# Twelve weight low parts move from GpSimd to VectorE, and VectorE's order changes in two mixers

## The reference, cut to what matters

```python
x = x + 0.5 * (silu(n @ w_gate) * (n @ w_up)) @ w_down   # n = rmsnorm(x), width 2816
p = rmsnorm(x) @ w_in
z = gelu(p[..., :512]); u, v = z[..., :256], z[..., 256:]
v = group_layernorm(v, v_norm, 4)                # 4 groups of 64
sv = einsum('gts,bnsgd->bntgd', w_s * tril, v) + b_s
y_a = u * sv
y_b = bg * shortconv(cg * xin)
y_c = silu(g) * group_layernorm(retention(rotary(q), rotary(k), v), gn, 4)
x = x + concat(y_a, y_b, y_c) @ w_out
x = x + 0.5 * swiglu(rmsnorm(x))                 # again width 2816
```

## Time and profile before

| what | value |
|---|---|
| median of 3 runs | 3357.05 us (3355.66 to 3357.43) |
| profiled execution, its own time | 3355.51 us |
| its span, first to last instruction | 3353.9 us |
| TensorE busy | 3236.1 us, 96% |
| VectorE busy | 2029.2 us, 61% |
| ScalarE busy | 1457.0 us, 43% |
| GpSimd busy | 906.4 us, 27% |
| mean granted TensorE clock | 0.992 |

### The profile page before, as it was taken

The page is one execution under the profiler, slowest core; times in us unless marked ns, Lnnn a source line. Parts: engine busy times, 40 slices in busy tenths (PEclk is TensorE's granted clock), DMA queues, the critical chain, the costliest instruction groups (busy, mean ns, idle before and its releaser), DMA issues.

```text
span 3353.9 us, 47772 instructions
## 1 busy us (share of the span) xinstructions
PE 3236.1 (96%) x20092; PEld 2874.7 (86%) x20092; DVE 2029.2 (61%) x2997; ACT 1457.0 (43%) x2244; POOL 906.4 (27%) x413
## 2 busy tenths in 40 slices
PE   8999999999989999999999999999999999999998
PEld 6887899978668899888999778899899998788998
DVE  6568755445856544575747636574775576366656
ACT  4465445433534444354434324453454343235433
POOL 3210133321400333203232431323232323313232
PEclk9999999999999999999999999999999999999999
DMA  4310333331102333313222322332332323223332
GB/s 131 112 43 26 107 97 117 103 100 58 63 26 88 101 113 101 124 56 123 89 88 95 113 84 77 117 101 82 114 101 86 105 85 122 76 89 107 94 96 76
DMA packets 239815, 308.97 MB, mean 92 GB/s; under 512 B 8337, under 2 KB 168097, under 8 KB 239089
## 3 DMA queue, kind: packets, MB, share of 16 engines
q1 hardware_dynamic: 236016, 291.41, 27.1%
q0 software_dynamic: 3584, 14.52, 1.2%
HBM read 303.80 MB, written 2.10 MB: 91 GB/s over the span
## 4 chain that ended last, share of the span: by engine, by line
PE 78%; DVE 16%; ACT 3%; issue 1%; DMA 0%; POOL 0%; DVEq 0%; ACTq 0%
PE bank L595 24%; PE bank L597 24%; PE bank L596 24%; DVE wlo L2074 3%; ACT whi L1318 1%; DVE wraw L2096 1%; DVE raw_w L2096 1%; PE bank L974 1%; DVE xl L2147 1%; PE bank L615 1%; PE bank L1257 1%; PE bank L1248 1%; DVE ul_w L2274 1%; PE bank L1182 0%; DVE st L2105 0%
## 5 line engine op out<-in xcount | busy, mean ns | idle before, releaser
L3128 POOL TENSOR_TENSOR wlo<-wraw,whi 128x1024 fp32r<-128x1024 f32 (+3 forms) x217 | 555.0, 2561 | 1508.0 <-ACT whi L1318 1507.6
L595 PE MATMUL bank<-xh,whi 128*128 128x256 f32 (+1 forms) x2456 | 724.6, 295 | 48.6 <-DVE zt L2269 20.0
L1318 ACT ACTIVATE whi<-wraw 128x1024 fp32r<-128x1024 f32 (+3 forms) x426 | 440.6, 1038 | 675.8 <-PE bank L597 545.2
L597 PE MATMUL bank<-xh,wlo 128*128 128x256 f32 (+1 forms) x2456 | 718.7, 293 | 0.0
L596 PE MATMUL bank<-xl,whi 128*128 128x256 f32 (+1 forms) x2456 | 715.3, 291 | 0.0
L595 PEld LDWEIGHTS bank<-xh,whi 128*128 128x128 f32 x2456 | 467.3, 190 | 69.9 <-issue 28.8
L3128 POOL TENSOR_TENSOR wlo<-raw_w,whi 128x1024 fp32r<-128x1024 f32 (+1 forms) x130 | 311.6, 2401 | 723.5 <-ACT whi L1318 723.5
L596 PEld LDWEIGHTS bank<-xl,whi 128*128 128x128 f32 x2456 | 468.0, 191 | 10.3
L597 PEld LDWEIGHTS bank<-xh,wlo 128*128 128x128 f32 x2456 | 466.5, 190 | 10.5
L595 PE MATMUL bank<-whi,uh_w 128*128 128x512 f32 x1216 | 473.9, 390 | 0.0
L597 PE MATMUL bank<-whi,ul_w 128*128 128x512 f32 x1216 | 473.4, 389 | 0.0
(11 more groups left out here) (392 smaller groups left out, 5049.0 us busy)
## 6 DMA issues: line engine op xcount, KB each, us to landing
wraw<-in_w_in SPq DMA_DIRECT2D x26, 1024.0 KB, 5.2
wraw<-in_ffn_w_down SPq DMA_DIRECT2D x20, 1024.0 KB, 5.1
raw_w<-in_ffn_w_down SPq DMA_DIRECT2D x20, 1024.0 KB, 5.1
raw_w<-in_mlp_w SPq DMA_DIRECT2D x19, 1024.0 KB, 5.1
wraw<-in_mlp_w SPq DMA_DIRECT2D x17, 1024.0 KB, 5.2
wraw<-in_ffn_w_gate SPq DMA_DIRECT2D x32, 512.0 KB, 4.8
raw_w<-in_ffn_w_gate SPq DMA_DIRECT2D x32, 512.0 KB, 5.0
raw_w<-in_ffn_w_up SPq DMA_DIRECT2D x32, 512.0 KB, 4.5
```

Source lines behind the costliest of these rows:

```text
L595: M.matmul(o, lh, rh, start=start, stop=False, skip_group_check=more)
L597: return M.matmul(o, ll, rh, start=False, stop=stop, skip_group_check=more)
L1318: A.activation(hi, raw, ACT.Copy).then_inc(*k.w_hi.inc(("hi", j)))
L3128: G.tensor_tensor(lo[:, 0:n], raw[:, 0:n], hi[:, 0:n].bitcast(F), ALU.subtract).then_inc(*k.w_lo.inc(("lo", j)))
```

## The change

Two things are changed.

In the first unit of each wide stage (`start and i == 0`), the low parts of the weights of p = 2 and p = 3 are put on VectorE. That is two items in each of six stages, twelve in all; other units are as before.

In the two layer mixers VectorE's order is changed: the triangle product goes in front of the statistics, the statistics wait for gelu token tile by token tile, with the four `bn_stats` of a tile in front of its four `bn_aggr` and one wait between them, and `gated(3)` is issued in front of the last step of the `("lg", l, 5)` block, `run(units)`. TensorE's program has the same swap, which there only moves the release of a PSUM bank.

```diff
-    def units(self, tag, keys):
+    def units(self, tag, keys, start=False):
...
-            u.items[p] = self.item(tag, u.loads[host], 1, 0, 4, "pool" if p in ON_POOL else "dve", u, p)
+            low = "pool" if p in ON_POOL and not (start and i == 0) else "dve"
+            u.items[p] = self.item(tag, u.loads[host], 1, 0, 4, low, u, p)
...
-            blocks["up", i, a] = plan.units("up", keys)
+            blocks["up", i, a] = plan.units("up", keys, a == 0)
...
-            blocks["glu", 2 * l + which, a] = plan.units("glu", keys)
+            blocks["glu", 2 * l + which, a] = plan.units("glu", keys, a == 0)
...
-        for i in range(16):
-            x = s.uv[:, i // 4, 256 + (i % 4) * 64:256 + (i % 4 + 1) * 64]
-            dve.wait_ge(at("gelu", l, 3))
-            V.bn_stats(st[:, i, 0, :], x).then_inc(*done.inc())
+        dve.wait_ge(at("ws", l))
+        V.tensor_tensor(s.wsr[:, :, :], s.wsr[:, :, :], bcast(con[:, C_TRI:C_TRI + 128], 4, 128), ALU.mult).then_inc(*done.inc(("wsr", l)))
+        for tt in range(NT):
+            dve.wait_ge(at("gelu", l, tt))
+            for i in range(4 * tt, 4 * tt + 4):
+                x = s.uv[:, tt, 256 + (i % 4) * 64:256 + (i % 4 + 1) * 64]
+                V.bn_stats(st[:, i, 0, :], x).then_inc(*done.inc())
             dve.wait_ge(done.now())
-            V.bn_aggr(mv[:, i, :], st[:, i, 0:1, :]).then_inc(*done.inc())
+            for i in range(4 * tt, 4 * tt + 4):
+                V.bn_aggr(mv[:, i, :], st[:, i, 0:1, :]).then_inc(*done.inc())
...
-        dve.wait_ge(at("ws", l))
-        V.tensor_tensor(s.wsr[:, :, :], s.wsr[:, :, :], bcast(con[:, C_TRI:C_TRI + 128], 4, 128), ALU.mult).then_inc(*done.inc(("wsr", l)))
...
         values(3)
+        gated(3)
         run(units)
-        gated(3)
```

## The result

The changed kernel takes 3339.69 us (median of 4 runs, 3339.38 to 3342.61). In the same session the kernel before takes 3356.55 us (4 runs, 3355.66 to 3357.43). The ratio is 0.9948, 95% interval 0.9936 to 0.9959: 16.9 us faster. The prediction was 3341.6 us, 15.4 us faster. The profiled executions differ by 15.7 us of span, 3353.9 against 3338.2, and it is those 15.7 us that the traces can account for.

What follows compares the result with a forecast made beforehand. TensorE, busy for 96% of the span, was taken to bound the kernel. Starts 8.4 us, mixers 1.2 and 2.8, and clock 3 make 15.4, from 3357.05 to 3341.6 us; range for 8 in 10 is 3336 to 3352.

Steps and rivals of the forecast that it cites:

- p = 2: First units: with its low part on VectorE, TensorE's wait before product 7 falls from 1.7 to 0.65 us.
- p = 3: First units: with both low parts on VectorE, product 4 starts 1.4 us earlier, 8.4 us over six stages.
- The clock: Behind glu-stage waits of 2.45 us: three of four falls to 1.2 GHz go, 3 us gained, bounds 0 and 4.
- Part two: Mixers, statistics and triangle product: first rotation 0.6 us earlier each, 1.2 us in all, stopped there by a GpSimd operation.
- Part three: Mixers, gated(3) issued earlier: `l_out` starts 1.4 us earlier each, 2.8 us in all, bounds 0.5 and 2.0 each.
- A: Rival: the lower clock stays after the glu waits of 2.1 us too, 3344.6 us; chance 0.17.
- B: Rival: the wide-stage starts give everything back, only the mixers' 4.0 us remain, 3353.0 us; chance 0.08.
- C: Rival: rotation slips ahead of GpSimd, 1.2 us more each, and all four clock falls go, 3338.2 us; chance 0.08.
- D: Rival: VectorE's stretches are not GpSimd's doing, added operations push product 4 back 2.3 us a stage, 3366.7 us; chance 0.05.

Runs made afterwards that it cites:

- p2_only: Changed kernel, but in each first unit only p = 2's low part is on VectorE, p = 3's on GpSimd; 3345.89 us.
- p3_only: Changed kernel, but in each first unit only p = 3's low part is on VectorE, p = 2's on GpSimd; 3349.5 us.
- sum_first: Changed kernel, with VectorE forming the sum of product 4 ahead of p = 3's low part in the first units; 3330.64 us.
- after_again: The changed kernel itself, run again beside three variants of it; 3342.53 us, ratio 0.9959 to the kernel before.
- ret_on_dve: Changed kernel, with the low parts of items 6 and 7 of l_ret on VectorE in both mixers; 3339.68 us.
- act_late: Changed kernel, with ScalarE's two weight splits at each mixer's end issued behind its first two copies of turned features; 3339.11 us.
- starts_only: Kernel before, with only the twelve low parts of the first units put on VectorE, mixers unchanged; 3345.83 us.
- dve_all: Changed kernel, with the low parts of p = 2 and 3 on VectorE in every unit, 112 more operations; 3360.87 us.
- mixers_only: Changed kernel, with the twelve low parts back on GpSimd, so only the two mixers have the new order; 3350.36 us.
- triangle_only: Kernel before, with only the triangle product moved in front of the statistics; 3354.41 us in one run.
- tiles_only: Kernel before, with only the statistics taken by token tile, the triangle product still behind them; 3356.12 us in one run.
- all_three: Changed kernel with the edits of sum_first, ret_on_dve and act_late together; 3327.24 us, ratio 0.9902 to the kernel before.

## Why the prediction was right, step by step

**p = 2.** Expected a sum of 1.2 us and a first wait of 0.65. Measured 1.22 and 0.65 in the changed kernel, 0.64 in p2_only. Right.

**p = 3.** Expected that the 2.90 us operation returns to 0.68, that product 4's low part comes 1.4 us earlier, and that the second wait is 2.1 us in glu and 1.35 in mlp. Measured 0.69, and 2.10 and 1.34. p2_only and p3_only show that its own share is 0.35 us. Right. The step also held that from the low part of product 4 on VectorE's queue runs without a gap, and that came too. Ahead of that low part stand 0.52 us of waiting for ScalarE. They are in the prediction's own times without being named (the operand's low part would end near 1506.9, the next starts at 1507.35), and sum_first turned them into time.

**The clock: the term that was mis-sized.** The prediction took 1.0 us for a fall and three of four gone, 3 us in all. The windows show 1.5 us for a fall (1.3 in the first glu stage), and two of four gone in the profile of the changed kernel: 2.8 us. In after_again only one is gone. So the term was right by two errors that cancel, which is luck. The size could have been read from the rows on record. The window of 3.00 us in the earlier trace rows holds 26 matmuls, not 24, so 48 of them take 48 x 2.99 / 26 = 5.5 us at full clock, and 7.05 - 5.5 is 1.5 us. The clock column says the same: 7.05 us at a mean of 0.79 is 1.5 us lost. A product was counted where the row counted matmuls. (In the changed kernel the same 48 take 5.73 us at a clock of 1.00. That is 1.3 us less, so both ways come out a little high for this stage.)

**Part two.** Expected 1.8 us left and 0.6 us gained in each mixer, bounded by GpSimd. Measured 1.83. The rotation's first operation, and GpSimd's in the first mixer:

```profile
1883.33 1.86 DVE L2344 TENSOR_TENSOR PT_x<-PT_x,k_x 128x256 f32<-128x256 f32 x1 [7.20 <-ACT PT_x L1508]
```

```profile
1882.50 2.41 POOL L3131 TENSOR_TENSOR wlo<-wraw,whi 128x1024 fp32r<-128x1024 f32 x1 [3.27 <-ACT whi L1319]
```

GpSimd started 0.83 us ahead and ended at 1884.91. VectorE's operation ends at 1885.19, the predicted 0.28 us behind it. ret_on_dve took GpSimd's operation away, and 1.2 us more went. The Trainium skill's rule in "SBUF — State Buffer", section "Who interferes with whom", that such a pair of instructions exclude each other for the whole instruction and the first to start wins, agrees with these rows and with that run.

**Part three.** Expected `l_out` 1.4 us earlier in each mixer and a new wait of about 0.7 us for line 2318's low part (2319 after). Measured: the wait of 2.0 us is gone, and the new one is 0.83. VectorE's timeline at the end of the first mixer, against the earlier trace rows:

```profile
1991.95 0.69 DVE L3073 TENSOR_TENSOR gs_x<-gs_x,ret_x 128x512 f32<-128x512 f32 x1
1992.61 0.69 DVE L3079 TENSOR_TENSOR yb_x<-yb_x,bank 128x512 f32<-128x512 f32 x1
...
1995.19 1.29 DVE L2319 TENSOR_TENSOR xl<-bank,xh 128x512 fp32r<-128x512 f32 x2 [1.89 <-ACT xh L1489]
```

Head 3's product is done ahead of the `lg` step and takes 0.69 us where it took 1.90. Act_late shows that the new wait is ScalarE's order: with the copy first it goes.

**The rivals.** A (the clock stays low) describes two of the four stages, and in after_again three. B fell with starts_only. C did not come: no rotation slipped ahead of GpSimd. D did not come: both stretches vanished with GpSimd's operations, so its condition, that they are not GpSimd's doing, did not hold. That added operations can push product 4 back showed in dve_all, in other units. By medians the gain of 16.9 us is 1.5 above the forecast, and in after_again, at 13.6, it is 1.8 below. What is shown of the 15.4 are the 12.4 us of waits; how near the total comes depends on which falls a run has.

## What to carry to other kernels

An operation moved from GpSimd to VectorE costs its own length on VectorE, and can still shorten VectorE's queue, when it takes away a stretch longer than itself; where no such stretch lies on the path (dve_all) the same move is a loss, and it can slide VectorE's other operations under GpSimd's that are left. So read each unit for itself. In a queue that works in order, put what another engine is waiting for ahead of what nobody waits for yet: sum_first swaps two operations, and its median is 11.9 us lower, of which waits account for 4.4. Cost a fall of the clock from equal stretches of equal work, with the matmuls counted in the row.

## What the runs showed of the hardware

**The clock behind a wait.** A fall to 1.2 GHz costs this kernel 1.5 us, 33.07 us against 31.58 for 264 matmuls. I counted over the profiles how many of the four glu starts were followed by one. Waits of 2.45 us (before, mixers_only, p2_only, triangle_only, tiles_only): 18 of 20. Waits of 2.1 us (after, after_again, starts_only, p3_only, ret_on_dve, act_late): 12 of 24. dve_all, with 2.1 us at these starts too, had 2 of 4. Waits of 1.4 us (sum_first, all_three): 0 of 8. At 2.1 us the same kernel had two in one profile and three in the next, so going from 2.45 to 2.1 us gave back some of the falls, and going to 1.4 all of them. What decides at 2.1 us is open, and length alone doesn't decide: the wait of 2.65 us near 1404.8 us was followed by a fall before and by none after.

**How much scatters.** The kernel before ran from 3355.44 to 3361.41 us on one chip, more than most terms of the sum. The waits at the places compared here repeat in the profiles to 0.05 us. The terms of 0.6 to 1.4 us were settled by waits, and only the sum by times; for mixers_only the two differ by 3.7 us.

**How long VectorE stands still.** Behind a GpSimd operation of 2.4 us a rotation operation of 128x256 ends 0.28 us after it (1884.91 to 1885.19), and a sum of 128x1024 ended 1.08 us after it. The low part with a PSUM source at 1995.19 to 1996.48, two operations in 1.29 us, is not stretched, though GpSimd works from 1993.81 to 1998.54.
